# Small 64x64 products over all four quarters of TensorE, in the chunk chains of a state-space block

## The chip, the cores and the metric

The program runs on one core of a Trainium2 chip. The metric is device time in microseconds (us) of one execution; each version is run several times and the median is compared. The core's engines work side by side, each through its own list of instructions in order, and wait for each other through semaphores. TensorE (PE in the profile) multiplies matrices and writes into PSUM, which has 8 banks of 128 partitions by 512 float32 numbers. VectorE (DVE) and ScalarE (ACT) do element-wise work and move results from PSUM to the on-chip memory SBUF. SyncE (SP) and GpSimd (POOL) issue transfers.

## The reference

Two transformer-like blocks run one after the other on a sequence of 512 positions of width 1024, all in float32: a first block (a convolution, a differential attention and a cross attention, merged by gates), and a second one, whose token mixer joins a gated spatial product and an RWKV-7 recurrence, followed by a feed-forward network. The change lies in the recurrence, which has 8 heads of 64 features:

```python
def _rwkv7_step(S, inp):
    r, w, k, v, a, b = inp
    sa = jnp.einsum('bhij,bhj->bhi', S, a)
    S = S * w[:, :, None, :] + sa[..., None] * b[:, :, None, :] + v[..., None] * k[:, :, None, :]
    y = jnp.einsum('bhij,bhj->bhi', S, r)
    return S, y
...
    S0 = jnp.zeros((B, B_HEADS, B_HEAD_DIM, B_HEAD_DIM), f32)
    _, y = lax.scan(_rwkv7_step, S0, xs)
```

The kernel does not step through 512 positions. It cuts the sequence into 8 chunks of 64, and brings each chunk of each head into closed form, for which it needs the inverse of a triangular 64x64 matrix (identity minus a strictly triangular one). It builds that inverse by doubling the size of the blocks that are already inverted, in levels 0 to 5.

## The kernel before

The large products of both blocks are on TensorE: a weight unit of 128x1024 arrives from memory, ScalarE rounds it (`weight_hi`), VectorE or GpSimd takes the rest (`weight_lo`), and `mm3` (L583 to L586) multiplies three times. This runs at nearly full TensorE use through most of the program.

The recurrence is in the middle of it. A *pair of heads* f (0 to 3) has 128 features on the partitions. It has 16 chunk matrices (2 heads by 8 chunks) of 64x64: one tile `[128, 8, 64]` holds them all, slot m = 4 * head + (pair of chunks), with the even chunk of the pair on partitions 0 to 63 and the odd one on 64 to 127. A product of two such tiles is 16 matmuls of 64x64. Each uses one *quarter* of TensorE's array: the half of the partitions that its operands lie on gives the rows, and the half of the partitions that its result goes to gives the columns.

`pe_chunks(f)` (L1326), `dve_chunks(f)` (L2740) and `act_chunks(f)` (L2070) are the three engines' parts of a chain:

- `matrices(source)` (L1331 to L1341): two times 16 matmuls of 64x128 give the products of the decayed vectors; VectorE masks them into `LM0` (source 0) and `LM1` (source 1), at L2745.
- Level l = 0 to 5. First V: TensorE puts an identity into every slot by one matmul of 128x128 by 128x512 (`ident_r` by `ident_2`, L1347), and adds 16 products of `LM0` and X (of `LM0` and the identity in level 0; L1288). VectorE multiplies the bank by the level's mask, into V (L2167; into X, which is half of the tile `AL`, in level 0). Then, in levels 1 to 4, `pe_level` (L1299) makes X = Y'V and Y = V'Y, 16 matmuls each, in turn, one quarter after the other, so that each pair's quarters are (rows, same half) and (rows, other half). ScalarE copies X (L2080), then Y (L2085) to SBUF. In level 5 there are the products `LkV` (`LM1` by the value tokens) and Y, one after the other.
- `GH`: 16 matmuls of 64x128 from Y and `AL` (L1386); half 0 is copied by ScalarE (L2088), half 1 by VectorE (L2776).
- `QP` (L1399) and `ZY` (L1412 to L1418): 16 matmuls of 64x128 and 64 of 64x64 for a pair of heads, which already spread over four quarters.

In the V products of all levels, in `LkV`, in the Y of level 5 and in `GH`, the rows and the columns of a matmul's quarter hang together in one fixed way, so only two of the four quarters work in them.

For level 0, VectorE makes Y from `LM0` by a mask (L2167) and adds the identity (L2763), both 128x512, the second waiting for the first.

PSUM: `wide` is a ring of seven banks (0, 1, 2, 4, 5, 6, 7). Each product takes the next bank of the ring and waits until that bank's last reader is done.

The order is written by hand in `rwkv_rounds` (L1477), which all three engines follow:

```python
interleave(chunks(0), chunks(1), itertools.chain(features(2), features(3)))
interleave(itertools.chain(tokens(2), tokens(3)), chunks(2), chunks(3), states(0), states(1))
interleave(states(2), states(3), out_steps())
```

`interleave` runs one piece of each (up to its `yield`) in turn. So in *round 1* two chains run beside the feature work of the next pairs of heads, which is mostly on VectorE and ScalarE. In *round 2* two more chains run beside the transposes (`tokens`, L1273, L1281) and the states of the first two (L1438 to L1460), whose last steps are wide float32 matmuls. *Round 3* goes back to weights. No weights are split or multiplied in rounds 1 and 2.

Of the kernel before, what the change touches and what calls it, by code (L numbers as in the profile page):

```python
# [8 lines left out]
FP32 = mybir.dt.float32  # L9
# [5 lines left out]
P = 128  # L15
# [222 lines left out]

class Count:
# [37 lines left out]
def build(nc, dram, out):  # L277
# [101 lines left out]
    ident_r = second("ident_r", [P, P], FP32R)  # L379
# [51 lines left out]
    banks = [nc.alloc_psum_tensor(f"bank{n}", [P, 512], FP32) for n in range(8)]  # L431
# [12 lines left out]
    wide = bank_ring((0, 1, 2, 4, 5, 6, 7))  # L444
    half_places, last_places = bank_ring((0, 1, 2, 3)), bank_ring((3, 4, 5, 6, 7, 0, 1, 2))
# [840 lines left out]
    def pe_square(pe, bank, lhs, rhs, m, rows, lanes, start=True):  # L1286

        return pe.matmul(bank[lanes, cut(m, CHUNK)], lhs(m, rows), rhs(m, rows), start=start, stop=start or m == 7)  # L1288

    def pe_squares(pe, bank, lhs, rhs, start=True, crossed=False, turned=False):  # L1290

        for m in range(8):
# [4 lines left out]
    def pe_level(pe, banks, Y, V, table, crossed):  # L1299

        for m in range(8):
            for part in range(2):
                rows = cut(part ^ crossed, CHUNK)
                x_done = pe_square(pe, banks[0], table(Y), table(V), m, rows, cut(part, CHUNK))
                y_done = pe_square(pe, banks[1], table(V), table(Y), m, rows, cut(1 - part, CHUNK))
        return x_done, y_done

    def chunk_parts(f):

        LM0, LM1 = work[f % 2][0:2]  # L1310

        def table(t):
            return lambda m, lanes: t[lanes, m, :]
# [7 lines left out]
        def identity(m, lanes):  # L1321
            return ident[lanes, lanes]

        return table, masked, rows_of, identity

    def pe_chunks(pe, f):  # L1326
        LM0, LM1, X, Y, V, AL = work[f % 2]
        K_tok, V_tok = tokens[f % 2]
        table, masked, rows_of, identity = chunk_parts(f)
# [15 lines left out]
        for level in range(6):  # L1345
            bank = wide.take(pe, ("V", f, level), dve_c, f, "V", level)
            pe.matmul(bank, ident_r[:, :], spread(ident_2[:, :], 8), start=True, stop=False)  # L1347
            if level == 0:
                pe.wait_ge(*dve_c.at(f, "masked", 0, 1))
            elif level == 1:  # L1350
                pe.wait_ge(*dve_c.at(f, "V", 0))
            else:
                pe.wait_ge(*act_c.at(f, "X", level - 1))
            pe_squares(pe, bank, masked(0, 0), table(X) if level else identity, start=False, turned=level > 1).then_inc(
                *pe_c.up(f, "V", level))
# [3 lines left out]
            if level == 0:  # L1359
                yield  # L1360
                continue
            if level < 5:
# [4 lines left out]
                x_done.then_inc(*pe_c.up(f, "X", level))  # L1367
                y_done.then_inc(*pe_c.up(f, "Y", level))
                yield
                continue  # L1370
            bank = wide.take(pe, ("LkV", f), act_c, f, "LkV")
            pe.wait_ge(*dve_c.at(f, "masked", 1, 1))
            pe.wait_ge(*act_f.at(f, "tok", 3))
            pe_squares(pe, bank, masked(1, 0), rows_of(V_tok)).then_inc(*pe_c.up(f, "LkV"))
# [8 lines left out]
        for m in range(8):  # L1383
# [3 lines left out]
            if m % TT == TT - 1:  # L1387
                done.then_inc(*pe_c.up(f, "GH", m // TT))
# [1611 lines left out]
```

## Time and profile before

| | us |
|---|---|
| median of 3 runs | 1618.45 |
| lowest and highest | 1614.27, 1621.84 |
| the profiled execution, its own time | 1617.28 |
| its span in the profile | 1615.6 |
| TensorE busy | 1563.6 (97%) |
| VectorE busy | 997.4 (62%) |
| ScalarE busy | 715.9 (44%) |
| granted TensorE clock, mean | 0.992 |

The profiled execution took 1.7 us more than its span. The chain of work that ended last lies for 69% on TensorE, for 21% on VectorE, for 6% on ScalarE, and for 3% it waits for nothing that the profile shows ("issue"). A float32 matmul stands in the trace as two records, each with a weight load (PEld) beside it; so 16 matmuls are "x32". The `fp32r` matmuls of L584 to L586 and of L1347 are one record each.

### The profile page before, as it was taken

To read this page: it belongs to the slowest core of one execution; us is meant where nothing else is said; L and a number is where in the kernel's file an instruction comes from. 1 tells how busy PE (TensorE), PEld (TensorE's weight loads), DVE (VectorE), ACT (ScalarE), POOL (GpSimd) and SP (SyncE) were. 2 spreads that over 40 slices of the span, in tenths; PEclk is the share of its full clock that TensorE was granted. 3 is DMA by queue.
4 is the path that set the end of the run, shared out by engine and by line. 5 is a ranking of instruction groups with operands and counts; after the bars stand their busy time and mean duration, and the time that the engine had idled before them with its cause. 6 is when DMAs were issued, how large, how long until landed. Compare 5 with 4: busy or idle time off the path is not lost.

```text
span 1615.6 us, 24372 instructions
## 1 busy us (share of the span) xinstructions
PE 1563.6 (97%) x9964; PEld 1254.6 (78%) x9964; DVE 997.4 (62%) x1684; ACT 715.9 (44%) x1151; POOL 190.3 (12%) x159
## 2 busy tenths in 40 slices
PE   7999999999999999999999999889999999999997
PEld 6878777888888777777887887668777887888886
DVE  6999995566555578667445748685447443334445
ACT  5544457345524477657532536553325222322112
POOL 2445464300010000000005000000000000000000
PEclk9999999999999999999999999999999999999999
DMA  6323243544564323232424232200012242333321
GB/s 214 103 88 122 92 144 105 195 144 137 150 199 131 122 88 101 68 105 92 140 95 152 75 102 79 78 3 4 3 53 102 85 126 86 97 91 103 93 91 53
DMA packets 45645, 166.07 MB, mean 103 GB/s; under 512 B 5264, under 2 KB 5392, under 8 KB 45536
## 3 DMA queue, kind: packets, MB, share of 16 engines
q1 hardware_dynamic: 42912, 155.95, 30.1%
q0 software_dynamic: 2624, 8.59, 1.9%
q8 instruction: 79, 1.29, 0.3%
q14 instruction: 30, 0.25, 0.1%
HBM read 162.42 MB, written 2.10 MB: 102 GB/s over the span
## 4 chain that ended last, share of the span: by engine, by line
PE 69%; DVE 21%; ACT 6%; issue 3%; DMA 0%; DVEq 0%; SPq 0%; ACTq 0%
PE bank L584 21%; PE bank L586 20%; PE bank L585 20%; DVE bank L2170 8%; PE bank L1288 2%; DVE weight_lo L634 1%; ACT weight_hi L626 1%; DVE scratch L2170 1%; ACT scratch L595 1%; DVE scratch L2167 1%; DVE small L2196 1%; DVE x_rows L2170 1%; ACT L595 0%; PE bank L1140 0%; ACT L590 0%
## 5 line engine op out<-in xcount | busy, mean ns | idle before, releaser
L626 ACT ACTIVATE weight_hi<-raw 128x1024 fp32r<-128x1024 f32 x237 | 250.3, 1058 | 526.4 <-PE bank L586 524.3
L584 PE MATMUL bank<-h_T_hi,weight_hi 128*128 128x512 f32 (+1 forms) x1184 | 476.9, 403 | 3.4 <-DVE scratch L2167 1.4
L634 DVE TENSOR_TENSOR weight_lo<-raw,weight_hi 128x1024 fp32r<-128x1024 f32 x180 | 220.3, 1226 | 403.3 <-ACT weight_hi L626 403.3
L586 PE MATMUL bank<-h_T_hi,weight_lo 128*128 128x512 f32 (+1 forms) x1184 | 463.1, 391 | 0.0
L585 PE MATMUL bank<-h_T_lo,weight_hi 128*128 128x512 f32 (+1 forms) x1184 | 461.6, 390 | 0.0
L584 PEld LDWEIGHTS bank<-h_T_hi,weight_hi 128*128 128x128 f32 x1184 | 223.6, 189 | 57.7 <-issue 8.6
L586 PEld LDWEIGHTS bank<-h_T_hi,weight_lo 128*128 128x128 f32 x1184 | 223.1, 188 | 50.1
L585 PEld LDWEIGHTS bank<-h_T_lo,weight_hi 128*128 128x128 f32 x1184 | 223.5, 189 | 48.6 <-issue 3.9
L2170 DVE SCALAR_TENSOR_TENSOR bank<-conv_in,columns,bank 128x512 f32<-128x512 f32 x240 | 181.4, 756 | 8.3
L634 POOL TENSOR_TENSOR weight_lo<-raw,weight_hi 128x1024 fp32r<-128x1024 f32 x57 | 140.0, 2458 | 153.1 <-ACT weight_hi L626 152.9
L584 PE MATMUL bank<-branch_hi,weight_hi 128*128 128x512 f32 x192 | 76.0, 396 | 0.1
L585 PE MATMUL bank<-branch_lo,weight_hi 128*128 128x512 f32 x192 | 75.5, 393 | 0.0
L586 PE MATMUL bank<-branch_hi,weight_lo 128*128 128x512 f32 x192 | 75.0, 390 | 0.0
L584 PE MATMUL bank<-weight_hi,hidden_hi 128*128 128x512 f32 x176 | 69.4, 394 | 0.0
L585 PE MATMUL bank<-weight_lo,hidden_hi 128*128 128x512 f32 x176 | 69.4, 394 | 0.0
L586 PE MATMUL bank<-weight_hi,hidden_lo 128*128 128x512 f32 x176 | 69.4, 394 | 0.0
L584 PE MATMUL bank<-weight_hi,h_T_hi 128*128 128x512 f32 x160 | 63.5, 397 | 0.0
L586 PE MATMUL bank<-weight_hi,h_T_lo 128*128 128x512 f32 x160 | 63.3, 396 | 0.0
L585 PE MATMUL bank<-weight_lo,h_T_hi 128*128 128x512 f32 x160 | 63.3, 396 | 0.0
L647 DVE SCALAR_TENSOR_TENSOR raw<-raw,silu_row 128x1024 f32<-128x1024 f32 x48 | 60.0, 1251 | 0.0
L595 ACT ACT_TABLE_LOAD x43 | 55.2, 1283 | 5.8 <-issue 2.6
L792 POOL DMA_DIRECT2D ln_rows<-in_ln_g x4 | 2.2, 547 | 380.8 <-DVE scratch L2167 307.0
(453 smaller groups left out, 2365.0 us busy)
## 6 DMA issues: line engine op xcount, KB each, us to landing
raw<-in_weights SPq DMA_DIRECT2D x289, 512.0 KB, 3.5
x_in<-in_x SPq DMA_DIRECT2D x4, 512.0 KB, 5.3
x_rows<-in_x POOLq DMA_DIRECT2D x4, 512.0 KB, 5.1
out<-x_rows SPq DMA_DIRECT2D x4, 512.0 KB, 2.6
mem_in<-in_mem POOLq DMA_DIRECT2D x2, 512.0 KB, 4.2
ln_rows<-in_ln_g POOLq DMA_DIRECT2D x4, 256.0 KB, 4.2
ln_rows<-in_ln_b POOLq DMA_DIRECT2D x4, 256.0 KB, 4.8
silu_row<-in_c POOLq DMA_DIRECT2D x1, 512.0 KB, 5.3
```

Of the source, the lines that this page charges most:

```text
L584: pe.matmul(o, lhs[0], rhs[0], start=start, stop=False)
L585: pe.matmul(o, lhs[0], rhs[1], start=False, stop=False)
L586: return pe.matmul(o, lhs[1], rhs[0], start=False, stop=stop)
L595: return act.activation(o, i, func, bias=bias, scale=scale)
L626: act.activation(weight_parts(u)[0][:, :], raw[u % RAW][:, :], ACT.Copy).then_inc(*weight_hi.up(u))
L634: engine.tensor_tensor(lo[:, :], raw[u % RAW][:, :], view(hi[:, :]), ALU.subtract).then_inc(*ready.up(u))
L647: dve.scalar_tensor_tensor(out=slot, in0=slot, scalar=1.0, in1=silu_row[:, :], op0=ALU.mult, op1=ALU.mult, accum_out=mod[:, v, k:k + 1]).t ...
L792: pool.dma_start(ln_rows[half][:, :], dram[f"{name}_g"][:, cut(half, 512)].broadcast_to([P, 512])).then_inc(*rows_loaded.up(name, half, 0))
L1288: return pe.matmul(bank[lanes, cut(m, CHUNK)], lhs(m, rows), rhs(m, rows), start=start, stop=start or m == 7)
L2167: return dve.tensor_tensor(o, a, b, ALU.mult)
L2170: return dve.scalar_tensor_tensor(out=o, in0=a, scalar=scalar, in1=b, op0=op0, op1=op1)
L2196: dve.bn_stats(found[:, 6 * n:6 * n + 6], source[:, cut(n, 512)]).then_inc(*dve_own.up())
```

## The change

Four parts, all in the chains.

1. **Four quarters for every product.** A pair of banks (`bank_pairs`, a new ring `wide_pairs` of three pairs: banks 0 and 1, 4 and 5, 6 and 7) takes the results. `pe_squares` goes through the 16 matmuls in groups of four, one in each quarter. For this, half of the results go to the other half of the partitions (`other_lanes`), and the slots of V, X and Y are put in another order from level to level.
2. **X ahead of Y.** Instead of `pe_level`, all 16 matmuls of X are issued, and then all 16 of Y.
3. **The identity once.** VectorE adds the identity to `LM0` once for each pair of heads (signal `unit`); the 24 matmuls of L1347 and `ident_r` are gone. Y of level 0 is then a mask alone, in one operation of 128x256 and two of 64x256.
4. **`GH` over four quarters.** Its second half comes from the odd slots, whose partitions are turned; ScalarE stores the first token tile in three pieces instead of one for that.

The copies and masks read the same number of elements from two banks that they read from one before.

```diff
+class PairRing:
...
+    def take(self, engine, use, signal, *key):
+        places, ap = self.pairs[self.uses % len(self.pairs)]
+        self.uses += 1
...
+        for place in places:
+            place.take(engine, signal, *key)
+        return ap
...
+    wide_pairs = PairRing([(bank_places[2 * n:2 * n + 2], bank_pairs[n][:, :, :]) for n in (0, 2, 3)])
...
+    def other_lanes(level, m):
+        token_bit, head_bit, pair_bit = m % 2, m // TT, m // 2 % 2
+        return (token_bit, token_bit ^ head_bit, token_bit, token_bit ^ head_bit, token_bit ^ head_bit ^ pair_bit, token_bit)[level]
...
+    def pe_squares(pe, pair, order, lhs, rhs, rows_turned, lanes_turned):
+
+        for n in range(4):
             for part in range(2):
-                done = pe_square(pe, bank, lhs, rhs, m, cut(part ^ crossed, CHUNK), cut(part ^ turned, CHUNK), start)
+                for group in range(2):
+                    m = order[4 * group + n]
+                    rows, lanes = cut(part ^ rows_turned(m), CHUNK), cut(part ^ lanes_turned(m), CHUNK)
+                    done = pe.matmul(pair[lanes, group, cut(n, CHUNK)], lhs(m, rows), rhs(m, rows), start=True, stop=True)
         return done
...
-            bank = wide.take(pe, ("V", f, level), dve_c, f, "V", level)
-            pe.matmul(bank, ident_r[:, :], spread(ident_2[:, :], 8), start=True, stop=False)
             if level == 0:
-                pe.wait_ge(*dve_c.at(f, "masked", 0, 1))
-            elif level == 1:
-                pe.wait_ge(*dve_c.at(f, "V", 0))
+                bank = wide.take(pe, ("V", f, level), dve_c, f, "V", level)
+                pe.wait_ge(*dve_c.at(f, "unit"))
...
+                pair = wide_pairs.take(pe, ("V", f, level), dve_c, f, "V", level)
+                pe.wait_ge(*(dve_c.at(f, "V", 0) if level == 1 else act_c.at(f, "X", level - 1)))
+                done = pe_squares(pe, pair, v_order(level), masked(0, 0), in_order(X, x_order(level - 1)), straight,
+                                  lambda m: other_lanes(level - 1, m))
+            done.then_inc(*pe_c.up(f, "V", level))
...
             if level < 5:
-                pair = wide.take(pe, ("X", f, level), act_c, f, "X", level), wide.take(pe, ("Y", f, level), act_c, f, "Y", level)
+                pair = wide_pairs.take(pe, ("X", f, level), act_c, f, "X", level)
                 pe.wait_ge(*(act_c if level > 1 else dve_c).at(f, "Y", level - 1))
                 pe.wait_ge(*dve_c.at(f, "V", level))
-                x_done, y_done = pe_level(pe, pair, Y, V, table, level > 1)
...
+                pe_squares(pe, pair, x_order(level), Y_before, V_l, before, straight).then_inc(*pe_c.up(f, "X", level))
...
+            pair = wide_pairs.take(pe, ("Y", f, level), act_c, f, "Y", level)
+            pe_squares(pe, pair, y_order(level), V_l, Y_before, before, after).then_inc(*pe_c.up(f, "Y", level))
             yield
...
         masks(0)
+        diagonals = LM0[:, :, :, 0:CHUNK].rearrange("p j n c -> p (j n) c")
+        dve.wait_ge(*dve_c.at(f, "masked", 0, 1))
+        dve.tensor_tensor(diagonals, diagonals, spread(view(ident_2[:, :]), 8), ALU.add).then_inc(*dve_c.up(f, "unit"))
         yield
...
             if level == 0:
-                mult(dve, Y[:, :, :], LM0[:, :, :, 0:CHUNK].rearrange("p j n c -> p (j n) c"), spread(levels[:, 0, :], 8)).then_inc(*dve_own.up())
-                dve.wait_ge(*dve_own.last())
-                dve.tensor_tensor(Y[:, :, :], Y[:, :, :], spread(view(ident_2[:, :]), 8), ALU.add).then_inc(*dve_c.up(f, "Y", 0))
+                by_token, small = diagonals.rearrange("p (n two) c -> p two n c", two=2), spread(levels[:, 0, :], 4)
+                mult(dve, Y[:, 0:4, :], by_token[:, 0], small)
+                for part in range(2):
+                    lanes, turned = cut(part, CHUNK), cut(1 - part, CHUNK)
+                    done = mult(dve, Y[turned, 4:8, :], by_token[lanes, 1], small[lanes])
+                done.then_inc(*dve_c.up(f, "Y", 0))
```

How TensorE's instructions move is seen best at levels 2 and 3 of round 1. In these rows AL holds X (it is the same tile), the numbers behind a tile tell the two chains apart, and "x16" is 16 matmuls. Before, from the V of level 2 of both chains to the first products of the first chain's X and Y, and then on:

```order
L1347 MATMUL bank<-ident_143,ident_r 128x512
L1288 MATMUL bank<-AL_169,LM0a 64x64 x16
L1347 MATMUL bank<-ident_143,ident_r 128x512
L1288 MATMUL bank<-AL_176,LM1a 64x64 x16
L1288 MATMUL bank<-V_167,Y_168 64x64
L1288 MATMUL bank<-Y_168,V_167 64x64
L1288 MATMUL bank<-V_167,Y_168 64x64
L1288 MATMUL bank<-Y_168,V_167 64x64
```

The same place in the changed kernel, to the end of that level, with what each instruction waits for:

```order
L1336 MATMUL bank<-V_166,Y_167 64x64 [waits chunk_act,chunk_dve]
L1336 MATMUL bank<-V_166,Y_167 64x64 x15
L1336 MATMUL bank<-Y_167,V_166 64x64 [waits chunk_dve]
L1336 MATMUL bank<-Y_167,V_166 64x64 x15
L1336 MATMUL bank<-V_173,Y_174 64x64 [waits chunk_act,chunk_dve]
L1336 MATMUL bank<-V_173,Y_174 64x64 x15
L1336 MATMUL bank<-Y_174,V_173 64x64 [waits chunk_act]
L1336 MATMUL bank<-Y_174,V_173 64x64 x15
L1336 MATMUL bank<-AL_168,LM0a 64x64 [waits chunk_act]
L1336 MATMUL bank<-AL_168,LM0a 64x64 x15
```

The identities are gone, X's 16 matmuls stand ahead of Y's, and with three pairs of banks the second chain's Y has a wait of its own: its pair is the one that the first chain's X was in, which ScalarE must have copied. The number of 64x64 matmuls is the same.

On VectorE, at the start of a chain in round 1, before:

```order
L2167 TENSOR_TENSOR LM0a<-bank,mask 128x4x128 [waits chunk_pe] x2
L2167 TENSOR_TENSOR LM1a<-bank,mask 128x4x128 [waits chunk_pe] x2
...
L2167 TENSOR_TENSOR Y_168<-LM0a,levels 128x512
L2763 TENSOR_TENSOR Y_168<-Y_168,ident_143 128x512 [waits dve_own]
```

and in the changed kernel:

```order
L2209 TENSOR_TENSOR LM0a<-bank,mask 128x4x128 [waits chunk_pe] x2
L2798 TENSOR_TENSOR LM0a<-LM0a,ident_142 128x8x64 [waits chunk_dve]
L2209 TENSOR_TENSOR LM1a<-bank,mask 128x4x128 [waits chunk_pe] x2
L2798 TENSOR_TENSOR LM1a<-LM1a,ident_142 128x8x64 [waits chunk_dve]
...
L2209 TENSOR_TENSOR Y_167<-LM0a,levels 128x256
L2209 TENSOR_TENSOR Y_167<-LM0a,levels 64x256 x2
```

The addition of the identity has moved from Y to `LM0`, ahead of level 0's products, which wait for it.

## Rows read from the trace of the kernel before

**Rows 1.** Windows by stage: round 1 and round 2.

```profile
core 0: us, PE busy (x) PEld busy (x) DVE busy (x) ACT busy (x) POOL busy (x), PEclk, DMA share, GB/s
1045.00:1103.00 58.00, 49.47 (x1568) 41.44 (x1566) 43.82 (x75) 30.32 (x52) 0.00 (x0) 0.97 0.04 12
1103.00:1165.00 62.00, 58.19 (x1695) 47.64 (x1693) 32.82 (x64) 23.47 (x46) 0.00 (x0) 1.00 0.02 4
```

**Rows 2.** Timeline of TensorE, level 1's last product and level 2's V (start us, us).

```profile
1064.26 0.22 PE L1288 MATMUL bank<-V,Y 64*64 64x64 f32 x1
...
1065.31 0.50 PE L1347 MATMUL bank<-ident,ident_r 128*128 128x512 f32 x1
1065.74 1.15 PE L1288 MATMUL bank<-AL,LM0a 64*64 64x64 f32 x32
1066.82 0.50 PE L1347 MATMUL bank<-ident,ident_r 128*128 128x512 f32 x1
```

**Rows 3.** The chain that ended last, in order of time (start us, us, what), rounds 1 and 2.

```profile
1088.26 1.28 DVE V L2167 x2
1092.11 3.57 PE bank L1386 x61
...
1139.43 0.70 DVE k_T L2167
1147.15 0.63 ACT y_b L2116
1148.32 1.15 PE bank L1288 x32
1153.96 3.27 PE bank L1386 x60
```

**Rows 4.** Timeline of VectorE in round 1: an idle time, Y of level 0, and two 128x256 operations.

```profile
1051.49 0.43 DVE L2687 TENSOR_SCALAR scratch<-scratch 128x512 f32<-128x512 f32 x1 [1.56 <-ACT scratch L595]
...
1055.62 0.68 DVE L2167 TENSOR_TENSOR Y<-LM0a,levels 128x512 f32<-128x512 f32 x1
1056.95 0.68 DVE L2167 TENSOR_TENSOR Y<-LM1a,levels 128x512 f32<-128x512 f32 x1
...
1097.67 0.75 DVE L2783 TENSOR_TENSOR P_T<-bank,P_T 128x256 f32<-128x256 f32 x2
1098.33 0.75 DVE L2786 TENSOR_TENSOR AR<-bank,AR 128x256 f32<-128x256 f32 x2
```

**Rows 5.** The page: instructions of each engine, and the transfers of instructions.

```profile
PE 1563.6 (97%) x9964; PEld 1254.6 (78%) x9964; DVE 997.4 (62%) x1684; ACT 715.9 (44%) x1151; POOL 190.3 (12%) x159
...
q8 instruction: 79, 1.29, 0.3%
```

**Rows 6.** Timeline of TensorE: two restarts, with the idle time before each.

```profile
1161.89 0.27 PE L1416 MATMUL bank<-LM0a,AL 64*64 64x64 f32 x2 [0.83 <-issue]
...
1165.48 0.27 PE L1416 MATMUL bank<-LM1a,AL 64*64 64x64 f32 x2 [1.46 <-issue]
```

**Rows 7.** Windows of 0.1 us in which 16 KB arrive (the last column, GB/s).

```profile
1090.70:1090.80 0.10, 0.10 (x17) 0.10 (x14) 0.00 (x0) 0.10 (x2) 0.00 (x0) 1.00 0.74 164
1103.10:1103.20 0.10, 0.10 (x1) 0.10 (x2) 0.00 (x0) 0.10 (x1) 0.00 (x0) 1.00 0.67 164
1113.50:1113.60 0.10, 0.10 (x2) 0.10 (x3) 0.10 (x1) 0.10 (x1) 0.00 (x0) 1.00 0.70 164
1137.90:1138.00 0.10, 0.10 (x2) 0.04 (x1) 0.00 (x0) 0.10 (x1) 0.00 (x0) 1.00 0.68 164
1147.10:1147.20 0.10, 0.10 (x13) 0.03 (x4) 0.02 (x1) 0.05 (x1) 0.00 (x0) 1.00 0.60 164
1163.10:1163.20 0.10, 0.10 (x21) 0.10 (x16) 0.00 (x0) 0.10 (x2) 0.00 (x0) 1.00 0.58 164
```

**Rows 8.** Windows around TensorE's long waits (columns as in the first group).

```profile
1062.00:1064.00 2.00, 2.00 (x66) 2.00 (x63) 1.93 (x3) 0.88 (x2) 0.00 (x0) 0.51 0.03 8
1163.00:1165.00 2.00, 1.01 (x69) 0.88 (x60) 0.00 (x0) 0.52 (x2) 0.00 (x0) 1.00 0.03 8
1167.00:1169.00 2.00, 2.00 (x8) 1.59 (x9) 1.59 (x9) 0.11 (x1) 0.00 (x0) 0.50 0.04 8
```

More of the change, by code:

```diff
@@ L429, in build @@
     last_squares = here("last_squares", [P, D])
-    banks = [nc.alloc_psum_tensor(f"bank{n}", [P, 512], FP32) for n in range(8)]
+    bank_pairs = [nc.alloc_psum_tensor(f"bank{n}", [P, 2, 512], FP32) for n in range(4)]
+    banks = [bank_pairs[n // 2][:, n % 2, :] for n in range(8)]
     bank_places = [Place(bank[:, :]) for bank in banks]
@@ new lines, in by_lanes, with v_order, x_order, y_order @@
+    def by_lanes(of):
+        return [m for group in range(2) for m in range(8) if of(m) == group]
+    def v_order(level):
+        return by_lanes(lambda m: other_lanes(level - 1, m))
+    def x_order(level):
+        return v_order(level) if level else list(range(8))
+    def y_order(level):
+        return by_lanes(lambda m: other_lanes(level - 1, m) ^ other_lanes(level, m) if level else other_lanes(0, m))
+    def in_order(t, order):
+        return lambda m, lanes: t[lanes, order.index(m), :]
@@ L1382, in pe_chunks @@
         pe.wait_ge(*act_c.at(f, "LkV"))
-        for m in range(8):
+        Y_last = in_order(Y, y_order(5))
+        for n in range(4):
             for part in range(2):
-                lanes = cut(part, CHUNK)
-                done = pe.matmul(pair[m // TT][lanes, cut(m % TT)], Y[lanes, m, :], AL[lanes, m, :, :], start=True, stop=True)
-            if m % TT == TT - 1:
-                done.then_inc(*pe_c.up(f, "GH", m // TT))
+                for half in range(2):
+                    m, rows = 2 * n + half, cut(part ^ half, CHUNK)
+                    done = pe.matmul(pair[half][cut(part, CHUNK), cut(n)], Y_last(m, rows), AL[rows, m, :, :], start=True, stop=True)
+                    if n == 3 and part == 1:
+                        done.then_inc(*pe_c.up(f, "GH", half))
         yield
@@ L2060, in act_tokens @@
             if n == 0:
-                o, bank = AL[:, :, 0, :].rearrange("p (j n) c -> p n j c", n=TT), bank.rearrange(by_head, j=2, c=CHUNK)
+                A_rows = AL[:, :, 0, :].rearrange("p (j n two) c -> p two n j c", j=2, two=2)
+                bank = bank.rearrange("p (n two j c) -> p two n j c", two=2, j=2, c=CHUNK)
+                for part in range(2):
+                    act.activation(A_rows[cut(1 - part, CHUNK), 1], bank[cut(part, CHUNK), 1], ACT.Copy)
+                o, bank = A_rows[:, 0], bank[:, 0]
             elif n == 1:
@@ L2775, in dve_chunks @@
         dve.wait_ge(*pe_c.at(f, "GH", 1))
-        dve.tensor_copy(AL[:, TT:2 * TT, :, :], wide["GH", f, 1].rearrange("p (m two c) -> p m two c", two=2, c=CHUNK)).then_inc(
-            *dve_c.up(f, "GH", 1))
+        dve.tensor_copy(AL[:, 1:8:2, :, :].rearrange("p m two c -> p m (two c)"), grid(wide["GH", f, 1])).then_inc(*dve_c.up(f, "GH", 1))
         yield
```

82 lines of the change are left out of this document (41 added, 41 removed).

## The prediction

> **What bounds the kernel now.** I read the page first: TensorE is busy for 97% of the span, so time taken from it counts, unless something else takes its place. Then the windows by stage [rows 1]. Rounds 1 and 2 are 58 and 62 us, 7% of the span, and all of the change is in them. In round 1 TensorE works for 49.5 of 58 us and VectorE for 43.8; in round 2 TensorE works for 58.2 of 62 and VectorE for 32.8. So round 2 looks bound by TensorE, and round 1 by a mixture. The chain of work [rows 3] agrees: in round 1 it goes for long stretches over VectorE's and ScalarE's feature work (the V masks at 1088.26 had waited for VectorE, not for TensorE), and in round 2 it stays on TensorE up to the variances, then goes over VectorE and ScalarE from 1139.43 to 1147.78, and back.
>
> A third view decides how much can be had: the supply of TensorE's own instructions. The page counts 9964 matmul and 9964 weight-load records and 79 transfers of instructions with 1.29 MB on TensorE's queue [rows 5]. That is 16.4 KB and 252 records a transfer, or 63 small float32 matmuls (two records of each kind). Twice in the last products of round 2 TensorE stood still for "issue", 0.83 and 1.46 us, and it restarted at 1161.89 and 1165.48 [rows 6]. So one transfer's worth of instructions took 3.6 us where nothing but their supply held it up. Small matmuls on four quarters use up as much in 2 us (below). The arrivals can be seen in windows of 0.1 us [rows 7]: three transfers from 1090.7 to 1103.1 (12.4 us), six from 1113.5 to 1137.9 (24.4 us), one from there to 1147.1 (9.2 us), and four up to 1163.1 (16.0 us). In the busy parts that is 4.1, 4.1 and 4.0 us for each, hardly above 3.6. The change takes only 24 matmuls of one record (48 records with their loads) out, and so less than one transfer.
>
> **The change, part by part.** First TensorE's time. The identity takes 0.43 us (1065.31 to 1065.74), and 16 matmuls on two quarters take 1.08 (1065.74 to 1066.82) [rows 2]. On four quarters 32 matmuls go from 1064.26 to 1065.31, which is 1.05, or 0.53 for 16.
> - The identities: 24 x 0.43 = 10.3 us.
> - V of levels 1 to 5 on four quarters: 20 x (1.08 - 0.53) = 11.0 us. Level 0 stays on two.
> - LkV and the last Y: 8 x 0.55 = 4.4 us.
> - GH: 3.57 and 3.27 us for two chains each [rows 3], halved: 3.4 us.
> - X ahead of Y frees nothing, but X is there 0.5 us earlier.
>
> Together 29.1 us of TensorE. Then what is added. VectorE: the identity onto LM0, 0.62 us and a wait of some 0.07, and for Y one operation of 128x256 and two of 64x256. Two of 128x256 take 0.66 (start to start) [rows 4], so three take 1.0, where mask and addition took 1.33 (1055.62 to 1056.95). That is +0.35 us for each pair of heads, 1.4 in all. A product of level 0 now waits for the added operation; it is hidden in round 1, where VectorE stands idle for 1.56 us up to 1051.49 [rows 4], and in round 2 it eats what the missing identity gives in level 0. ScalarE gets two more pieces for each pair of heads, at most 0.6 us each (a full one), off the chain. The shape of 64 partitions is not in the trace: nothing less than half of a 128x256 one and nothing more than a whole seems possible, and I take the whole.
>
> What of the 29.1 us lies on the path:
> - Round 1 before 1090: only at levels 3 and 4 does the path lie on V. Two identities and two V (2 x 0.98) are the upper bound, nothing the lower, and I take 1.0.
> - 1090.7 to 1103.1: three transfers cannot be used up in less than 3 x 3.6 = 10.8, so of 12.4 us 1.6 can go. GH, QP and ZY alone would give 1.7.
> - 1113.5 to 1137.9: six transfers, 21.6 of 24.4 us: 2.8, where TensorE's own time (three levels of 1.96) would give 5.9. I take off 0.5 for the new wait of the second Y on the copy of the first X: 2.3.
> - 1137.9 to 1147.1: VectorE and ScalarE, from the normalised rows to y_b [rows 3]: nothing.
> - 1147.1 to 1163.1: four transfers, 14.4 of 16.0 us: 1.6.
>
> That makes 6.5 us. Against it stands the clock. After TensorE had waited 3.0 us, the stretch from 1062 to 1064 has a granted clock of 0.51, and from 1167 to 1169, after stretches in which it was busy for half of the time, it is 0.50 [rows 8]; that is 1.2 GHz instead of 2.4. Two such microseconds cost one. In the new kernel TensorE waits for instructions where it worked before, so more of such stretches must be expected. I take two, of 2 us of work each, at 1 us: -2.0. The bounds are none, and most of both rounds (the rival below). "TensorE: Matmul & The Clock Gate" in the Trainium skill (HAM oscillation) likewise warns that a matmul loop with waits between its bursts falls back to the half clock again and again; it speaks against a change that makes bursts shorter, and the rows at 0.50 bear it out.
>
> Net 4.5 us. The profiled execution took 1617.3 us, so 1612.8; the median of the runs is 1.2 above it, so **1614.0**.
>
> **Rivals.**
> - **The supply is no limit** (0.22): transfers could come earlier when instructions are used up faster. For it: the arrivals are regular even where TensorE is slow. Against it: the two restarts 3.6 us apart. Then round 1 gives 3, since GH comes in whole; the three levels in the middle of round 2 give 5.9, less 0.6 for the copies; and the end of it 3.5 (two identities and V's, 2.0, LkV and Y 2.2, GH 1.6, less 2.3 for masks and copies that lie open). Together 11.8: 1606.7.
> - **Copies and masks take the place** (0.13). The mask of V, X's copy and Y's copy are as long as before, and with three pairs of banks instead of seven banks the second Y waits for the first X to be copied. Where ScalarE is in the middle of other work (until 1147.78 at level 4 [rows 3]) TensorE stands still with a product that it had behind it before. At 0.8 us (a V mask or copy of 0.6 and the wait) in six levels that is 4.8 of the 6.5: 1.7 us are left, 1616.8. "TensorEngine Tiling (Array Packing)" in the Trainium skill (PSUM Bottleneck) has this as a rule: after a tiled speedup the copies out of PSUM may be the bottleneck. No row here shows it yet, since VectorE is half idle in round 2.
> - **The quarters do not overlap as planned** (0.07). In Y's new order the row halves of neighbouring slots alternate, so a quarter can be asked for again two matmuls later. Halfway back to two quarters, Y takes 0.8 instead of 0.53; 20 x 0.27 = 5.4 us of TensorE, of which half on the path: 2.7 from 4.5, 1616.6.
> - **The half clock spreads: slower** (0.05). If TensorE is judged idle through whole levels, the wide float32 matmuls of the states and features run at half speed too. TensorE's work in both rounds is then 107.7 - 29.1 = 78.6 us; a fifth of it at half clock costs 15.7, and 6.5 - 15.7 = -9.2: 1627.6. It decides from 6.5 us of such work on.
>
> **How the numbers follow.** The forecast has 0.53, and its own range is 1611 to 1617 (supply interval 3.3 to 3.7, none to three clock stretches). With most of the first rival, the second and the third, 1605.5 to 1619 holds 0.8. About 0.5% (8 us) is what a measurement of this kernel can tell from no change. Faster than 1610.4 is most of the first rival (0.18) and a tail of the forecast (0.07): 0.25. Slower than 1626.5 is the last rival, 0.04. The rest, 0.71, is the same.
>
> **What would show it.** A V of levels 1 to 5 must show its 32 records in about 0.55 us, GH's 64 in 1.8, and L1347 must be gone. If I am right, TensorE's busy time in rounds 1 and 2 falls by over 20 us, its idle time "issue" rises to 10 us or more, and the arrivals of 16 KB are 3.6 us apart through most of round 2. If arrivals come closer than 3.3 us, my supply limit is wrong and the first rival holds. If the new idle time is put down to ScalarE's X copies, it is the second. A granted clock near 0.5 in several windows between 1115 and 1135 would be the last. The stages of weights before and after must be as long as they were.

## The result, and the profile after

The changed kernel takes 1623.65 us (median of 14 runs, 1621.79 to 1629.32) against 1617.9 us for the kernel before (14 runs, 1614.27 to 1621.84): a ratio of 1.0042, 95% interval [1.0031, 1.0053]. That is 5.7 us slower, where 4.5 us faster was forecast. It is within the 0.5% (8 us) that the prediction counts as no change, but clear of zero, on its other side, and above the range from 1611 to 1617. The profiled execution has a span of 1620.8 us.

The page's engines and its instruction transfers, to be laid beside [rows 5]:

```profile
PE 1545.6 (95%) x9940; PEld 1239.0 (76%) x9940; DVE 999.7 (62%) x1692; ACT 718.7 (44%) x1158; POOL 190.3 (12%) x159
...
q8 instruction: 79, 1.29, 0.3%
```

TensorE lost the 24 identities and works 18.0 us less (1563.6 before), VectorE 2.3 us more. Yet the span is longer. The windows by stage, as in [rows 1]:

```profile
1045.00:1103.00 58.00, 39.91 (x1494) 34.42 (x1492) 45.69 (x79) 31.51 (x55) 0.00 (x0) 0.88 0.04 12
1103.00:1165.00 62.00, 48.32 (x1505) 37.67 (x1496) 31.94 (x63) 24.11 (x48) 0.00 (x0) 0.97 0.01 3
1165.00:1200.00 35.00, 30.71 (x441) 21.63 (x441) 13.20 (x38) 8.23 (x16) 0.00 (x0) 0.95 0.05 17
```

TensorE is busy for 9.6 and 9.9 us less in the windows of the two rounds, so round 2 is not bound by it any more: 48.3 of 62 us. The granted clock fell from 0.97 to 0.88 in round 1 and from 1.00 to 0.97 in round 2. And the work no longer fits into the windows. Read from the timeline of TensorE by places that both kernels have (the first V of level 0 in a round, the first record of GH, LM of round 2, and the first product that reads y_b after the rounds), the stages are:

| stage, us | before | after | identity part alone |
|---|---|---|---|
| levels of round 1, V of level 0 to GH | 42.4 | 43.9 | 42.0 |
| GH to LM of round 2 | 12.8 | 12.7 | 12.7 |
| levels of round 2, V of level 0 to GH | 45.3 | 50.7 | 43.9 |
| GH to the first product with y_b | 35.4 | 34.1 | 32.2 |

The last column is the second of the experiments below. The loss is in the levels, above all in those of round 2. The stages of weights are as long as before: the first LM starts at 1047.1 us (1046.3 before), and from the first product with y_b to the end it is 425.6 us (426.5 before). The longest of TensorE's waits from 1045 to 1178 (line, releaser: us in total, times, longest):

```profile
PE bank L1336 <- issue: 5.5, 7, 1.8
PE bank L1373 <- DVE V L2209: 4.7, 1, 4.7
PE bank L1454 <- issue: 3.3, 2, 1.8
PE bank L1336 <- DVE V L2209: 3.0, 3, 2.2
PE bank L1336 <- ACT AL L2121: 1.9, 3, 1.3
PE bank L1498 <- DVE V L2209: 1.9, 1, 1.9
PE bank L1485 <- issue: 1.6, 1, 1.6
PE bank L1386 <- DVE LM1a L2798: 1.6, 2, 0.8
```

L1336 is every small square, L1373 is LM, L1386 V of level 0, L1454 part of ZY, L1498 the gate, L1485 the sum over the chunks ("later"). Waits put down to "issue" come to 11.5 us here, against 4.8 in the kernel before. Two of the others make no sense by the data. LM of source 1 reads k_T and AR and has nothing to do with V, nor has the gate. They wait for a bank. The timeline of TensorE at the first of them:

```profile
1055.97 0.69 PE L1336 MATMUL bank<-AL,LM0a 64*64 64x64 f32 x32 [1.34 <-DVE AL L2209]
1056.48 0.65 PE L1336 MATMUL bank<-AL,LM1a 64*64 64x64 f32 x32
1061.80 1.98 PE L1373 MATMUL bank<-AR,k_T 64*64 64x128 f32 x32 [4.67 <-DVE V L2209]
1063.56 1.08 PE L1336 MATMUL bank<-V,Y 64*64 64x64 f32 x32
```

The two V are issued in 1.16 us together: 0.58 each, four quarters at work, as planned (1.08 before [rows 2]). Then TensorE stands for 4.67 us, since LM's turn in the ring of seven is bank 1, half of the pair in which V of level 1 waits for its mask. And the work after it runs at half speed (this LM takes 1.98 us, the next 1.07). In the kernel before, TensorE waited 3.0 us for the same mask, but with LM already done.

The chain that ended last, in order of time, shows what came before the gate in round 2:

```profile
1135.12 0.63 DVE k_T L2850
1135.75 0.09 issue
1135.85 1.16 PE bank L1336 x64
...
1146.51 0.61 DVE k_T L2209
1147.13 0.03 issue
1147.15 0.56 DVE k_T L2858
1147.71 0.02 issue
1147.73 0.04 DVE k_T L2860
1147.77 0.57 issue
1148.34 0.69 DVE V L2209
1149.04 0.04 issue
1149.08 2.50 PE bank L1498 x4
```

V of level 3 (1135.85) starts when VectorE has added "later" (L2850), whose bank its pair shares. The second gate (1149.08) starts when V of level 4 has been masked (1148.34), and that mask stands in VectorE's queue behind the normalised rows (L2209, L2858, L2860). Nothing in the data asks for either: "later" of the two pairs of heads lies in banks 0 and 1, which are the pair of V of level 3, and the second gate's turn is bank 0, half of the pair of V of level 4.

### The profile page after: what moved, and what is told of

Its sections match the earlier page's. It is cut to its first block, busy times and chain, and to the rows that moved or that the text cites. A ratio compares the mean times of both kernels' runs of the same rounds, so it can differ in the third digit from the quotient of the medians.

```text
span 1620.8 us, 24387 instructions
## 1 busy us (share of the span) xinstructions
PE 1545.6 (95%) x9940; PEld 1239.0 (76%) x9940; DVE 999.7 (62%) x1692; ACT 718.7 (44%) x1158; POOL 190.3 (12%) x159
## 4 chain that ended last, share of the span: by engine, by line
PE 65%; DVE 25%; ACT 6%; issue 4%; DMA 0%; SPq 0%; DVEq 0%; ACTq 0%
PE bank L608 20%; PE bank L609 19%; PE bank L610 19%; DVE bank L2212 11%; PE bank L1336 1%; DVE weight_lo L658 1%; ACT weight_hi L650 1%; ACT scratch L619 1%; DVE scratch L2212 1%; DVE scratch L2209 1%; DVE small L2238 1%; DVE x_rows L2212 1%; PE bank L1164 0%; ACT L614 0%; ACT small L619 0%
```

## The experiments

Each time stands beside the kernel before on the same chip. "Levels" are the stages of the table above.

**1. Is the supply of instructions a limit?** The kernel before, with the products ZY of the last pair of heads issued nine times.

```diff
-        for first, second in (("BH", "KV"), ("HR", "VR")):
+        for first, second in (("BH", "KV"), ("HR", "VR")) * (9 if f == 3 else 1):
```

> The kernel before, in which the 64 small products ZY of the last pair of heads are issued nine times instead of once (same operands, same results). It measures the supply of instructions by itself. Supply theory: each repetition is one transfer of instructions (16 KB), which takes 3.6 us, so 8 x 3.6 = 28.8 us more than before (1646.7), with idle time put down to issue of about 14 us in that stretch. Rival (the supply follows demand; four quarters run at the 29 ns a product that ZY shows in its short bursts): 8 x 1.9 = 15 us more (1633).

Measured: 1646.98 us (one run), where the supply theory said 1646.7. The longest of TensorE's waits in the repeated stretch (11.3 us, where about 14 was expected):

```profile
PE bank L1417 <- issue: 11.3, 8, 1.9
```

Transfers of 16 KB arrive there 3.6, 3.5, 3.7, 4.2, 3.4, 4.2, 3.3, 3.4 and 3.4 us apart. So the limit is real: in this stretch small float32 products on four quarters are used up faster than their instructions come, 3.3 to 4.2 us (3.6 on average) for 252 records.

**2. The identity alone.** The kernel before, with the identity added to LM0 once on VectorE and no identity products; all else as it was (seven single banks, X and Y interleaved).

```diff
-            pe.matmul(bank, ident_r[:, :], spread(ident_2[:, :], 8), start=True, stop=False)
...
+        dve.tensor_tensor(diagonals, diagonals, spread(view(ident_2[:, :]), 8), ALU.add).then_inc(*dve_c.up(f, "unit"))
```

> The kernel before with the third part of the change alone: the identity added on VectorE, no L1347 matmuls, everything else on two quarters and single banks. Supply theory: it takes 10.3 us of TensorE work without making the small matmuls denser, so it should give 1 to 3 us less than before (about 1616). Rival (the loss of the changed kernel comes from the added operation ahead of level 0): 1 us slower or more (1619 to 1620).

Measured: 1612.47 us, ratio 0.9968 [0.9957, 0.9979]: 5.3 us faster, better than expected. So this part of the change is good by itself, and the rest of it costs 1623.6 - 1612.5 = 11 us. By the table, the levels gave 0.4 and 1.4 us and the stage behind GH 3.2. In the profiled execution of the kernel before, that stage ran at half clock for a while [rows 8]; here it does not:

```profile
1166.00:1168.00 2.00, 2.00 (x18) 1.39 (x19) 1.76 (x10) 0.00 (x0) 0.00 (x0) 1.00 0.00 0
1168.00:1170.00 2.00, 2.00 (x20) 1.39 (x20) 0.52 (x3) 0.00 (x0) 0.00 (x0) 1.00 0.03 8
```

The clock is not where the 5.3 us come from, though. The mean granted clock of all executions is 0.9932 here and 0.9936 in those of the kernel before beside it, and in this profile the levels of round 1 have more half clock than before.

**3. The pairs of banks alone.** The kernel before, in which V, X, Y and LkV each take a pair of banks out of three pairs and use one of the two; products, quarters and identities as before.

```diff
-            bank = wide.take(pe, ("V", f, level), dve_c, f, "V", level)
+            bank = (wide_pairs if level else wide).take(pe, ("V", f, level), dve_c, f, "V", level)
```

> The kernel before, in which V, X, Y and LkV take a pair of banks each as in the change, but use one bank of it, on two quarters as before. Bank theory: three pairs shared with the ring of single banks make TensorE wait for masks and copies (the products of source 1 wait for V's mask of level 1, the second Y for the first X's copy), 3 to 6 us slower than before (1621 to 1624). Supply theory alone: no change (1618), since the instructions are the same.

Measured: 1642.23 us, ratio 1.0153 [1.0139, 1.0167]: 24.5 us slower, far beyond what either theory said. The levels take 55.0 and 60.2 us. It is harsher than the change, since X and Y are interleaved here and both must have a pair before either can start, so its 24.5 us are no measure of what the pairs cost in the change; but it shows that banks alone can cost more than all that was to be gained:

```profile
PE bank L1312 <- ACT AL L2104: 8.4, 6, 3.2
PE bank L1312 <- DVE LM0k L2191: 3.0, 2, 1.5
PE bank L1363 <- DVE V L2191: 2.8, 1, 2.8
```

**4. V with half of its order undone.** The change, in which V of levels 1 to 5 issues the eight products of its first bank before those of the second. Each bank of a pair has the products of one couple of quarters, so only two quarters work at a time.

```diff
+            steps = [(n, part, group) for group in range(2) for n in range(4) for part in range(2)]
```

> The changed kernel with V's 16 matmuls issued in the order that uses two quarters at a time; banks, slots and waits are the change's. Supply theory: V's four quarters gain next to nothing, since the instructions come no faster: within 2 us of the changed kernel (1622 to 1626). Rival (four quarters do gain, and something else loses): 20 x 0.55 us of TensorE come back, of which half on the path, 5 us or more slower than the changed kernel (1629).

Measured: 1626.88 us, ratio 1.006 [1.0046, 1.0073], 3.2 us more than the change (the two intervals overlap a little), and between what the two theories said. The edit did less than I had meant: the V of two chains take 1.56 us together (1122.33 to 1123.89), 0.78 each against 0.58 in the change, not 1.08. Where products on one couple of quarters are followed by products on the other, their records lie side by side in the trace: those of the second chain's V begin at 1122.92, among the last of the first. The edit adds 20 x 0.2 = 4 us of TensorE's work, and by the medians 3.2 of them are paid. In a kernel whose TensorE waits so much, that is a high price, and it speaks for V being on the chain.

**5 and 6. Other orders of the banks.** The change, with the ring of seven and the three pairs in another order, and not one instruction more or less. The two kernels differ from the change only so:

```diff
-    wide = bank_ring((0, 1, 2, 4, 5, 6, 7))
+    wide = bank_ring((7, 5, 0, 6, 2, 1, 4))
-    wide_pairs = PairRing([(bank_places[2 * n:2 * n + 2], bank_pairs[n][:, :, :]) for n in (0, 2, 3)])
+    wide_pairs = PairRing([(bank_places[2 * n:2 * n + 2], bank_pairs[n][:, :, :]) for n in (3, 0, 2)])
```

```diff
-    wide = bank_ring((0, 1, 2, 4, 5, 6, 7))
+    wide = bank_ring((0, 1, 4, 5, 6, 7, 2))
```

> The change, with the seven single banks taken in the order 7, 5, 0, 6, 2, 1, 4 and the three pairs in the order (6,7), (0,1), (4,5). Not one instruction is added or taken away, only which bank a product goes to, and so which earlier reader it must wait for. Bank theory (a good part of the 11 us between this change and the identity part alone is products that wait for a bank whose last product is still being read): on paper the places where a bank is asked for within about four products of its last use grow by a third, so slower than the change's 1623.6 by 2 us or more, 1626 to 1631. Supply theory (TensorE waits for its own instructions): 1622.5 to 1625.

> The same as the run before, but with the single banks in the order 0, 1, 4, 5, 6, 7, 2, in which on paper a bank is asked for a little later after its last use than in the change (an eighth less). Bank theory: 1 to 2 us faster than the change, 1621.5 to 1622.5. Supply theory: 1622.5 to 1625.

Measured: 1631.34 us, ratio 1.0083 [1.0065, 1.0100], and 1629.84 us, ratio 1.0073 [1.0056, 1.0090]. Both are 6 to 8 us slower than the change. So which bank a product gets is worth more than everything that the change meant to gain; but my count of places on paper didn't tell a good order from a bad one: the "best" ring was to win 1 to 2 us and lost 6. Its levels take 44.2 and 55.0 us. Both also have a lower clock: 0.9875 and 0.9885 on average over all executions, 0.9901 in the change.

**7. Do the identities keep the clock up?** The change, with one dead 128x512 product of the identity into bank 3 ahead of each V of levels 1 to 5. (Where bank 3 has a reader left, the dead product waits for it.)

```diff
+                pe.matmul(banks[3], ident_r[:, :], spread(ident_2[:, :], 8), start=True, stop=True)
```

> The change, with one dead product of the identity (one 128x512 matmul, 0.43 us, into bank 3, that nobody reads) issued ahead of V of the levels 1 to 5 of every pair of heads: 20 x 0.43 = 8.6 us of work more on TensorE. Clock theory (the removed identities kept TensorE busy, and without them it falls to half clock around 1058 to 1066, 1092 to 1100 and 1150 to 1154 us): fewer stretches at 0.5, and a time no longer than the change's, 1620 to 1624. If the clock is only a symptom: the fillers lie in waits in part, so 1625 to 1630.

Measured: 1631.63 us, ratio 1.0086 [1.0068, 1.0105]: 8.0 us slower for 8.6 us of dead work. The mean granted clock of all executions did not gain (0.9897, against 0.9901), and in the profile it stands at half in the same places of round 1:

```profile
1060.00:1062.00 2.00, 0.08 (x4) 0.08 (x7) 2.00 (x4) 0.00 (x0) 0.00 (x0) 0.50 0.00 0
1062.00:1064.00 2.00, 2.00 (x44) 2.00 (x48) 1.93 (x4) 0.00 (x0) 0.00 (x0) 0.50 0.04 8
...
1094.00:1096.00 2.00, 2.00 (x51) 1.56 (x53) 1.06 (x3) 0.00 (x0) 0.00 (x0) 0.50 0.00 0
```

The stretch at half clock from 1150 to 1154 us is gone, but there is a new one from 1075 to 1079. In the identity part alone (run 2) the identities are gone as well, and the clock is that of the kernel before. So the theory that the missing identities cost the clock falls. And work just ahead of V is paid almost in full: TensorE's waits are no reserve into which it can go.

**8. Four quarters without pairs.** The identity part alone, and V of level 5 (off-diagonal quarters, one bank) issued in turns with LkV (diagonal quarters, another bank).

```diff
+                        v_done = pe_square(pe, bank, masked(0, 0), table(X), m, cut(part, CHUNK), cut(1 - part, CHUNK))
+                        l_done = pe_square(pe, other, masked(1, 0), rows_of(V_tok), m, cut(part, CHUNK), cut(part, CHUNK))
```

> The identity part alone (1612.5), and in addition V of level 5 and LkV of the same pair of heads issued in turns, V on the off-diagonal quarters into its bank, LkV on the diagonal ones into another: four quarters without pairs of banks and without other lanes. It frees 4 x 0.55 = 2.2 us of TensorE. Supply theory: half of it comes back, 1611 to 1612. If single banks and four quarters work without loss: 1610 to 1611. If V of level 5 comes too late now, for it ends with LkV: 1613 to 1614.

Measured: 1610.26 us, ratio 0.9960 [0.9947, 0.9973]. The levels take 39.9 and 43.2 us, and in the profiled execution no microsecond of the rounds has a clock under 0.95. It is 2.2 us under the identity part alone by the medians, less than the intervals can tell, and these two are the fastest versions of this study, ahead of both given kernels.

**9 and 10. LM off the pairs' banks.** The change, with LM of source 1 on banks 2 and 3, which no pair uses; once for all pairs of heads (`source`), once for the first (`source and f == 0`).

```diff
+    small_banks = bank_ring((2, 3))
...
+            ring_of = small_banks if source else wide
+            pair = [ring_of.take(pe, ("LM", f, source, j), dve_c, f, "masked", source, j) for j in range(2)]
```

> The change, with the eight products LM of source 1 (k_T with AR, two a pair of heads) on banks 2 and 3, which no pair uses, instead of the ring of seven. In the change the first of them stands 4.7 us for the mask of V of level 1 (its bank 1 is half of V's pair), and the runs with other rings have 5.3 and 5.6 us there. Bank theory: this wait goes, and with it 3 to 6 us: 1618 to 1621. Rival (the wait only moves, since X of level 1 waits for the same mask): 1622.5 to 1625. If the clock or the supply is all that matters: 1622.5 to 1625 too.

> As the run before, but only LM of source 1 of the first pair of heads (f = 0) goes to banks 2 and 3, the other three pairs stay in the ring, which is thereby moved on by two places after it. Bank theory: the wait of 4.7 us goes and 2 to 4 us with it, unless the moved ring makes another wait: 1619.5 to 1622. Rival: 1622.5 to 1625, or up to 1631 where the moved ring decides, as in the two runs before.

Measured: 1622.67 us, ratio 1.0031 [1.0020, 1.0042], and 1631.84 us, ratio 1.0084 [1.0067, 1.0101]. The first is 1 us under the change, less than the intervals can tell. The wait of 4.7 us at LM is gone in both and has moved, as the rival said. In the first of the two:

```profile
PE bank L1337 <- DVE V L2211: 6.8, 4, 3.9
PE bank L1337 <- ACT AL L2123: 3.2, 4, 2.0
```

X of level 1 now waits for the same mask (3.9 us), behind VectorE's feature work. That this wait was the price of the shared bank is refuted. The levels of round 2, though, took 47.1 us in the first and 57.6 in the second, where the gate waits 3.2 us for V's mask (1.9 in the change). The first run had 3.6 us less there than the change, but from GH to LM of round 2 it took 15.7 us instead of 12.7.

**11 and 12. Round 2's single products off the pairs' banks.** The first of the two runs before, with "later", the means, variances and gates of the first two pairs of heads on banks 2 and 3 as well; and the same with LM left in the ring.

```diff
+    def late_banks(f):
+        return small_banks if f < 2 else half_places
...
-        bank = state_banks(f).take(pe, ("gate", f), dve_s, f, "y")
+        bank = late_banks(f).take(pe, ("gate", f), dve_s, f, "y")
```

> The run with LM on banks 2 and 3, and in addition the sum over the chunks ('later'), the means, the variances and the gates of the first two pairs of heads on banks 2 and 3, so that no single product of round 2 but the state steps and the tokens shares a bank with a pair. In the change V of level 3 waits 0.76 us for a bank that 'later' holds until VectorE has added it, and the gate stands 1.9 us for the mask of V of level 4, which lies in VectorE's queue behind the work on the states. Bank theory: both waits go, and the levels of round 2 (first V at level 0 to GH), 50.7 us in the change and 47.1 with LM on free banks, come down to 44 to 46: 1619 to 1621. Rival (the chain V, mask, X, copy over VectorE's and ScalarE's queues sets the time, whatever the banks): 1622 to 1624.

> As the run before, but LM of source 1 stays in the ring of seven, so that round 1 is the change's, instruction by instruction and bank by bank. Bank theory: the wait of 1.9 us before the gate and the 0.76 us before V of level 3 go, the levels of round 2 from 50.7 to 47 to 49: 1620 to 1622.5. Rival: 1622.5 to 1625. If round 2 comes out near 55 us again as with the other rings, the order in which products of the chains and of the states meet VectorE's queue decides, and not these two banks: 1627 to 1632.

Measured: 1618.13 us, ratio 0.9998 [0.9988, 1.0009], and 1621.84 us, ratio 1.0018 [1.0007, 1.0029]. The levels of round 2 come down to 45.9 and 46.6 us, about where the bank theory had them, and the whole is 5.5 and 1.8 us faster than the change, by nothing but other banks. (The second profile is of an execution of 1617.27 us, 4.6 under that run's median, so its 46.6 may flatter it.) Taking products out of the ring of seven also moves all others in it to other banks. The traces show that the two waits at which the edit aimed are gone; that it was these, and not the new order of the rest, that gave the 5.5 us is not shown. From 1134 to 1152 us TensorE waited 1.9 us for V's mask before the gate and 0.8 us for "later" in the change; in the first of these two runs, all its waits there are:

```profile
PE bank L1490 <- issue: 1.3, 1, 1.3
PE bank L1337 <- DVE V L2214: 0.5, 1, 0.5
PE bank L1337 <- ACT AL L2126: 0.5, 1, 0.5
```

And now the supply shows. Windows of 0.1 us with an arrival of 16 KB, in that run, the first and the last of seven; the five between are at 1125.6, 1129.7, 1133.2, 1136.9 and 1140.3:

```profile
1121.80:1121.90 0.10, 0.10 (x19) 0.10 (x10) 0.10 (x1) 0.10 (x1) 0.00 (x0) 1.00 0.79 164
1144.10:1144.20 0.10, 0.10 (x2) 0.00 (x0) 0.00 (x0) 0.10 (x1) 0.00 (x0) 1.00 0.69 164
```

Six transfers in 22.3 us, 3.7 each. The change took 25.2 us for six in the same place (1118.8 to 1144.0), 4.2 each, and the kernel before 4.1 (24.4 [rows 7]). So with the banks out of the way this part of round 2 runs near the pace that I had taken for its floor. The levels as a whole do not: they are 45.9 us, and in the identity part alone 43.9, with six transfers in 23.9 us (1115.7 to 1139.6).

**13. Chain or supply.** The run with all single products on free banks, and V in the order of the fourth run, bank after bank: more time in each V, not one instruction more.

> The run with all single products of round 2 on banks 2 and 3 (1618.1), and V of the levels 1 to 5 with all products of its first row half issued before those of the second, as in the earlier run on V, where this made one V 0.76 us instead of 0.57: 20 x 0.2 = 4 us more of TensorE's work, all of it on the chain V, mask, X, copy of its pair of heads; not one instruction more. Chain theory (with the banks out of the way the chains of waits still set the time): 3 to 4 us slower, 1621 to 1622. Supply theory (what is left is the arrival of TensorE's instructions, which doesn't change): at most 1 us slower, 1618 to 1619.

Measured: 1619.17 us, ratio 1.0012 [1.0002, 1.0023]; that is 1 us slower by the medians and 2.2 by the ratios, and the intervals overlap: it does not decide between the two theories. The stages say more, in one profiled execution each. The levels of round 2 went from 45.9 to 46.0 us (nothing of the 2 us added there), and the arrivals of instructions stayed at 3.8 us on average (1119.6 to 1142.4): there V's time was free. The levels of round 1 went from 43.7 to 45.1 us, but they also have more half clock, 4.0 us against 2.6 by the count of the next section, and that alone makes the 1.4 us. Whether V's time is paid in round 1 is not shown.

## Why the prediction was wrong

- **The quarters overlap: right.** V takes 0.58 us; GH of round 2 has its 64 records in 2.01 us in the chain (1.8 expected, 3.27 before [rows 3]). GH of round 1 takes 3.67, with a granted clock of 0.50.
- **The freed 29.1 us: too much.** From the same place to the same place (1045 to 1166 before, 1045.8 to 1173.6 after) TensorE's busy time fell from 108.2 to 92.4 us, 15.8. Part of what was freed came back as time at half clock, where the same products keep TensorE busy for longer.
- **The supply limit: right in kind and size, wrong as the only limit.** The transfers that were to come every 3.6 us came every 3.3 to 4.2 where nothing else held TensorE up. The issue waits came as forecast, 11.5 us against 10 or more. But through the levels of round 2 in the change the transfers stayed 4.2 us apart, and not 3.6: something slower ruled.
- **The step that failed: "1113.5 to 1137.9 ... I take off 0.5 for the new wait of the second Y on the copy of the first X: 2.3".** The prediction asked only which pair holds up which other pair. Three pairs take six of the ring's seven banks, and all single products (LM, "later", gate) still go round that ring. So such a product can wait for a mask or copy of a chain with which it has nothing to do, and a V for a single product; since TensorE works in order, the wait holds up all that stands behind it. The levels of round 2 took 5.4 us more, not 2.3 less. Moving single products to two free banks changed nothing but banks; it took 4.8 us out of the levels of round 2 (1.7 us of half clock there in both), and 5.5 us out of the whole. That banks are worth this much is shown, and it is half of the 11 us between the whole change and its identity part. How much of it is the price of the shared places and how much is the luck of an order is open: three other orders (runs 5, 6 and 10) cost 6 to 8 us more.
- **The rival "copies and masks take the place" (0.13)** was right in kind. It had the three pairs instead of seven banks, but its price, 0.8 us in six levels, counted waits of the chains alone and stopped at 1616.8. (Its sum also leaves out the 2.0 us for the clock that the forecast has; with them it would be 1618.8.)
- **The identities.** They were right to take out: 5.3 us by themselves, for 10.3 us of TensorE's work. TensorE does stand still for the added operation, 0.8 us in each round (1.6 on L1386, in the identity part alone too). But VectorE, which comes next, gets to its masks no later: in round 1 it starts the masks of V of level 1 12.8 us after those of LM0 in both kernels (before, then after), and in round 2 10.0 us after them, where it was 9.8.

```profile
1047.45 1.29 DVE L2167 TENSOR_TENSOR LM0a<-bank,mask 128x512 f32<-128x512 f32 x2 [0.69 <-PE bank L1339]
1060.27 1.28 DVE L2167 TENSOR_TENSOR V<-bank,levels 128x512 f32<-128x512 f32 x2
...
1048.26 1.29 DVE L2209 TENSOR_TENSOR LM0a<-bank,mask 128x512 f32<-128x512 f32 x2 [0.69 <-PE bank L1373]
1056.43 1.28 DVE L2209 TENSOR_TENSOR Y<-LM0a,levels 128x256 f32<-128x256 f32 x3
1057.74 1.29 DVE L2209 TENSOR_TENSOR Y<-LM1a,levels 128x256 f32<-128x256 f32 x3
1061.06 1.28 DVE L2209 TENSOR_TENSOR V<-bank,levels 128x512 f32<-128x512 f32 x2
```

- **VectorE's small operations: under-sized.** The three pieces of Y were to take 1.0 us and take 1.31 (1056.43 to 1057.74), as long as mask and addition took before (1.33). The two on 64 partitions take 0.42 us each, and so does the one on 128. Cutting Y into three saved nothing, and VectorE works 2.3 us more in all, where 1.4 was expected. In the identity part alone, where Y is one mask, VectorE reaches V's masks of level 1 after 11.7 us instead of 12.8.
- **The clock: right in sign, and under-sized.** If each microsecond of the rounds and of what follows (1044 to 1200) counts with busy time times (1 - granted clock), half clock takes 4.6 us in the profiled execution before, 7.8 in that of the change, 5.6 in the first run on free banks, 3.3 with the identity part alone, none in the eighth run, and 15.0 in the tenth, the slowest ring. That is 3.2 for 2.0, and all executions together say more. Their mean granted clock is 0.9938 for the kernel before and 0.9901 for the change; time times (1 - clock) is 10 us and 16 us. The difference of 6 us is an upper bound of the cost, since it counts idle time too, but it is as large as the whole loss. Waits and clock go together here: in the change one stretch at half clock begins within the wait of 4.67 us, and another within a wait of 1.1 us before GH of round 1, soon after one of 2.2 us. The windows of the change at that GH, at full clock before:

```profile
1092.00:1094.00 2.00, 0.86 (x41) 0.75 (x34) 1.38 (x4) 1.93 (x4) 0.00 (x0) 0.60 0.00 0
1094.00:1096.00 2.00, 2.00 (x55) 2.00 (x52) 0.72 (x2) 1.28 (x3) 0.00 (x0) 0.50 0.04 8
1096.00:1098.00 2.00, 2.00 (x47) 2.00 (x43) 0.69 (x1) 0.60 (x1) 0.00 (x0) 0.50 0.00 0
```

  The passage of the Trainium skill that the prediction cited ("TensorE: Matmul & The Clock Gate", HAM oscillation) agrees with these traces: TensorE waits more often in the rounds, and half clock (1.2 GHz) takes 7.8 us instead of 4.6.

**What stays open.** The version on free banks is as fast as the kernel before, and 5.7 us behind the identity part alone, though TensorE has less to do in it. Of that 2.3 us are half clock by the count from the profiles; by the mean clock of all executions (0.9904 against 0.9932) it is up to 4.7 us. So the free banks gave back waits and hardly any clock, and why every version with pairs of banks has a mean clock of 0.991 or less, while those without have 0.993 or more, no run takes apart. For the rest, the waits on X's copies are 6.0 us against 4.3; no run parts that from X ahead of Y, nor from the added pieces on ScalarE and VectorE. That TensorE's gain was worth nothing in the levels of round 2 once the banks were free rests on the arrivals and on one profile of the last run; for round 1 it is open.

## What to carry to other kernels

Count banks as you count cycles: a product that takes two banks to run on four quarters takes them away from every product in the same ring, and an in-order engine turns a wait for an unrelated bank into a wait of all that is behind it. Before spreading small products over more quarters, see how far the supply of instructions is from the pace you want: here six transfers shrank from 24.4 to 22.3 us at best, and taking work out (the identities) gave what the spreading did not. Pairing two products that lie on different quarters anyway, each in its own bank (V beside LkV), at least cost nothing. Judge a change of several parts by each part alone: one of these four, the identity, was worth 5 us and the others together lost 11. And compare the granted clock over all executions, not in one profile: here one profile of each showed half of what the clock may have cost (3.2 of up to 6 us).

## What the hardware showed

- Small float32 products on four quarters run out of instructions: nine times in a row 16 KB, 252 records, took 3.3 to 4.2 us to arrive, while the two V of a level use 128 matmul and load records in 1.16 us.
- The same instructions with other banks differ by 8 us (1623.6 against 1631.3), and by 13.7 us between the best and the worst arrangement (1618.1 and 1631.8); the worst also has the lowest clock (0.985, against 0.990).
- Two runs of products on other quarters overlap at their seam by themselves: V on two quarters at a time, first one couple, then the other, takes 0.78 us, not 1.08.
- A VectorE product of 64 partitions by 256 elements took 0.42 us, as one of 128 partitions by 256 did, both from SBUF; one of 128 by 512 took 0.68.
